# Attention with the projections inside its steps: the job order of the first layer's mixer

## The chip, the cores and the metric

The kernel runs on one NeuronCore of a Trainium2 chip, as one program that computes three layers for one sequence of 256 tokens. The metric is the device time of one execution in microseconds (us). The engines are named as in the profile: PE is TensorE (matrix products, with PEld for its weight loads), DVE is VectorE, ACT is ScalarE, POOL is GpSimd, and SP is SyncE, which here only issues transfers. All data are 32-bit floats; each matmul of the source is two matmul instructions in the trace, a transpose is one.

## What is computed

Only the first layer's mixer is touched. Its input is 256 x 1024, and one input matrix of 2840 columns gives all queries, keys, values and gates:

```python
def nsa_moba_mixer(x, positions, w_in, w_out, ...):
    proj = x @ w_in
    qa, kc, vc, ksl, vsl, kw, vw, ga, qm, km, vm = jnp.split(proj, EVEN_SPLITS, axis=-1)
    qa, kc, ksl, kw = (rope(...) for ...)              # 8 query heads, 2 key heads each
    gates = jax.nn.sigmoid(ga)                         # three a head
    o_a = nsa_attention(...)                           # o = g0 * o_cmp + g1 * o_slc + g2 * o_win
    o_b = moba_attention(rope(qm), rope(km), vm)       # 8 heads
    return jnp.concatenate([o_a, o_b], axis=-1) @ w_out
```

In nsa_attention, o_cmp attends to 15 compressed keys for each of two key heads, gelu((blocks + pos) @ w1) @ w2 over blocks of 32 tokens with a stride of 16. At 256 tokens the selected blocks, the sliding window and the block attention (moba) all come out as causal attention over all keys. So there are 24 causal attention jobs of 64 channels: 8 selected (slc), 8 sliding (win) and 8 block (moba). The mixer's output is added to alpha times its input and normalised; a mixture of experts (MoE) follows, and then two more layers with their own mixers and experts.

## The kernel before

**Weights.** SP streams all weights through six slots of 16 KB a partition (slot, free_slot, load_cols, load_out). Chunk n goes to slot n % 6 and may be loaded when chunk n - 6 has been used, which PE tells by chunk_done. Chunks 0 to 5 are the columns of w_in: 0 the NSA queries, 1 the keys and values kc, vc, ks, vs, 2 the window's keys and values and the gates (280 columns), 3 moba's queries, 4 its keys, 5 its values. Chunk 6 is the two compression matrices w1 (CMP_CHUNK, four DMAs with pieces of 512 B), 7 and 8 the two column halves of w_out, and from 9 on the experts of the first MoE. Between chunks 5 and 6, SP issues all the small parameters.

**Banks.** PSUM has eight banks of 128 x 512. project(n, ...) fills two of the banks 4 to 7, one for each tile t of 128 tokens, 8 products deep (KT = 8). ACT copies them out (take), DVE rotates queries and keys (rope), PE transposes them (tr, into banks 0 to 3), and ACT copies the transposed heads into qk. cmp_hidden forms the hidden layer of the compression.

**Attention.** The helper attention(jobs, first, pairs0, extras) is written once for each engine and goes through steps s = 0, 1, ... In step s, PE computes the scores of job s (bank s % 2), runs extras[s] if there is one, transposes the probabilities of job s - 3 (bank 2 or 3), and in every second step multiplies two jobs' probabilities by their values (bank 4 or 5 by the pair). DVE takes job s's masked minimum, scales job s - 1 by the inverse sum and the gate, and copies a pair's finished output to mixT. ACT computes the exponentials of job s and copies the transposed probabilities of job s - 3. Each engine works its list in order. AB_JOBS has the 8 moba jobs first, then slc and win, four jobs of a pair in a row; mixT tiles 0 to 3 are of the slc and win pairs, 4 to 7 of moba. The extras are the compression branch, which needs banks 6 and 7: hidden layer at step 2, its gelu, transpose, keys, scores at step 8, softmax, transpose at step 11. After the attention, project_out multiplies mixT by w_out into banks 4 to 7, and mixer_residual on DVE adds, takes the statistics and normalises.

**What orders PE.** First the input is transposed and projections 0 to 2 run; then tr(0) to tr(3), projection 3, tr(4), projection 4, the moba transposes, projection 5, the 28 steps, project_out. Projections 3, 4 and 5 stand between the NSA heads and the first step:

```python
project(3, 512, 3)
tr(4, [pj[:, t, C_KW:C_KW + P] for t in range(T)])
project(4, 512, 4)
project(5, 512, 5, moba_keys)
pe.wait_ge(qt_act, 7)
attention(AB_JOBS, 0, 0, {2: cmp_hidden, 6: cmp_hiddenT, 7: cmp_keys, 8: cmp_score, 11: cmp_transpose})
```

## Time and profile before

| | |
|---|---|
| median of 3 runs | 1370.96 us (1368.24 to 1385.06) |
| the profiled execution | 1370.9 us, span 1369.1 us |
| its mean granted TensorE clock | 0.932 of full speed |
| PE busy | 1240.8 us (91% of the span) |
| DVE, ACT busy | 319.1 us (23%), 204.4 us (15%) |
| HBM read | 362.60 MB, 266 GB/s over the span |
| chain that ended last | PE 73%, DMA 18%, DVE 4%, issue 2%, ACT 2% |

The page gives one profiled execution: busy time of each engine, the span in 40 slices of 34.2 us, the chain of work that ended last, the costliest groups. The trace behind it answers by stretch (windows), in order of time (timeline) and by what an engine waited for. PE's matmuls are pipelined and their ends are modelled, so a row's own duration overlaps the next by a little; the distance between two starts is what a piece of work takes. Between 0 and 203 us of the span lies the first mixer.

### The profile page before, as it was taken

The page shows a single profiled execution, that of the slowest core. Times are in us where ns is not written, and L with a number is a line of the kernel's source. Part 1 is how long each engine was busy: PE and PEld are TensorE (multiplying, and loading weights), DVE is VectorE, ACT ScalarE, POOL GpSimd, SP SyncE. Part 2 cuts the span into 40 slices and gives each one's busy share as a digit, 9 for nine tenths or more (in the row PEclk, how much of TensorE's full clock was granted, in tenths as well). Part 3 has the DMA queues.
Part 4 walks back from the last instruction along what each step waited for, and adds up shares of the span by engine and source line. Part 5 has one row for each costly group of instructions (what it writes and reads, how often), then busy time and mean ns, then how long its engine had stood idle before and what let it go on. Part 6 is the DMA issues. An engine that isn't in the chain of part 4 may idle for free.

```text
span 1369.1 us, 14568 instructions
## 1 busy us (share of the span) xinstructions
PE 1240.8 (91%) x5882; PEld 623.1 (46%) x5882; DVE 319.1 (23%) x891; ACT 204.4 (15%) x468; POOL 0.7 (0%) x5
## 2 busy tenths in 40 slices
PE   6999998999999998999799879898898999889885
PEld 3546546554477746554364454532242232233221
DVE  1324633121300534111502263510010010000002
ACT  2023502110101612010112122100000000000000
POOL 0000000000000000000000000000000000000000
PEclk9997798999999898999999958899999999999998
DMA  9772022999934011999653300269999999999993
GB/s 351 144 295 105 1 70 95 408 415 395 333 128 176 9 62 67 404 418 403 232 176 126 145 1 15 109 270 428 428 425 429 429 429 428 428 427 427 428 427 161
DMA packets 76872, 364.38 MB, mean 266 GB/s; under 512 B 21234, under 2 KB 26644, under 8 KB 52116
## 3 DMA queue, kind: packets, MB, share of 16 engines
q1 hardware_dynamic: 75876, 361.93, 66.3%
q10 hardware_dynamic: 944, 1.73, 0.4%
q8 instruction: 36, 0.59, 0.2%
q14 instruction: 16, 0.13, 0.0%
HBM read 362.60 MB, written 1.05 MB: 266 GB/s over the span
## 4 chain that ended last, share of the span: by engine, by line
PE 73%; DMA 18%; DVE 4%; issue 2%; ACT 2%; SPq 0%; DVEq 0%; ACTq 0%
DMA weights<-in_expert_w_down_dram 17%; PE bank L649 13%; PE bank L926 13%; PE bank L966 8%; PE bank L675 6%; PE bank L664 6%; PE bank L959 5%; PE bank L990 4%; PE bank L898 2%; PE bank L901 2%; PE bank L732 1%; PE bank L866 1%; PE bank L706 1%; DMA weights<-in_ab_w_in_dram 1%; PE bank L692 1%
## 5 line engine op out<-in xcount | busy, mean ns | idle before, releaser
L926 PE MATMUL bank<-weights,projected 128*64 128x256 f32 (+1 forms) x2048 | 344.2, 492 | 18.7 <-DMA weights<-in_expert_w_gate_dram 9.2
L926 PEld LDWEIGHTS bank<-weights,projected 128*64 128x64 f32 (+1 forms) x2048 | 135.1, 124 | 213.3 <-issue 170.0
L649 PE MATMUL bank<-weights,x_transposed 128*128 128x512 f32 (+1 forms) x416 | 178.9, 589 | 9.6 <-DMA weights<-in_ab_w_in_dram 6.3
L966 PE MATMUL bank<-weights,work 128*32 128x512 f32 x512 | 121.4, 629 | 30.3 <-DMA weights<-in_expert_w_down_dram 30.3
L649 PEld LDWEIGHTS bank<-weights,x_transposed 128*128 128x128 f32 x416 | 79.6, 194 | 101.5 <-issue 96.1
L966 PEld LDWEIGHTS bank<-weights,work 128*32 128x32 f32 x512 | 35.4, 115 | 113.8 <-issue 112.5
L675 PE MATMUL bank<-weights,mixed 128*128 128x512 f32 x192 | 83.2, 594 | 1.6 <-DVE mixed L1695 1.1
L664 PE MATMUL bank<-x_transposed,weights 128*128 128x256 f32 (+1 forms) x352 | 76.4, 379 | 0.0
L1881 DVE COPY work<-bank 128x512 f32<-128x512 f32 (+1 forms) x32 | 22.1, 690 | 209.8 <-PE bank L966 140.4
L664 PEld LDWEIGHTS bank<-x_transposed,weights 128*128 128x128 f32 (+1 forms) x352 | 63.8, 182 | 13.0 <-issue 1.3
L959 PE MATMUL bank<-weights,work 128*32 128x512 f32 x512 | 63.3, 626 | 1.6 <-DVE work L1886 1.6
L990 PE MATMUL bank<-work,heads_transposed 128*128 128x512 f32 x128 | 63.7, 620 | 0.0
L1901 DVE TENSOR_TENSOR work<-work,bank 64x512 f32<-64x512 f32 (+1 forms) x24 | 16.4, 682 | 187.1 <-PE bank L926 187.1
L1376 ACT ACTIVATE work<-bank 128x512 f32<-128x512 f32 (+1 forms) x32 | 19.0, 594 | 265.0 <-PE bank L966 195.0
L675 PEld LDWEIGHTS bank<-weights,mixed 128*128 128x128 f32 x192 | 36.2, 190 | 47.0 <-issue 44.5
L1271 ACT ACTIVATE projected<-bank 128x512 f32<-128x512 f32 (+1 forms) x34 | 18.1, 583 | 191.2 <-PE bank L649 140.2
L990 PEld LDWEIGHTS bank<-work,heads_transposed 128*128 128x128 f32 x128 | 21.0, 188 | 43.0 <-issue 38.3
L1886 DVE COPY work<-bank 128x256 f32<-128x256 f32 (+1 forms) x24 | 12.2, 509 | 114.7 <-PE bank L938 114.7
L1386 ACT ACTIVATE work<-bank 64x512 f32<-64x512 f32 (+1 forms) x24 | 14.1, 589 | 159.9 <-PE bank L926 159.9
L959 PEld LDWEIGHTS bank<-weights,work 128*32 128x32 f32 x512 | 14.9, 113 | 41.5 <-issue 38.8
L898 PE MATMUL bank<-heads_transposed,projected 128*128 128x128 f32 x256 | 31.9, 279 | 0.0
L901 PE MATMUL bank<-heads_transposed,projected 128*128 128x256 f32 x128 | 29.2, 382 | 3.0 <-issue 2.7
(282 smaller groups left out, 990.0 us busy)
## 6 DMA issues: line engine op xcount, KB each, us to landing
weights<-in_expert_w_gate_dram SPq DMA_DIRECT2D x32, 2048.0 KB, 15.6
weights<-in_expert_w_up_dram SPq DMA_DIRECT2D x32, 2048.0 KB, 17.3
weights<-in_expert_w_down_dram SPq DMA_DIRECT2D x32, 2048.0 KB, 17.2
weights<-in_moe_w_gate_dram SPq DMA_DIRECT2D x16, 2048.0 KB, 10.7
weights<-in_moe_w_up_dram SPq DMA_DIRECT2D x16, 2048.0 KB, 12.9
weights<-in_moe_w_down_dram SPq DMA_DIRECT2D x16, 2048.0 KB, 9.8
weights<-in_sb_w_in_dram SPq DMA_DIRECT2D x6, 2048.0 KB, 18.3
weights<-in_w_in_dram SPq DMA_DIRECT2D x6, 2048.0 KB, 15.0
```

Of the source, the lines that this page charges most:

```text
L649: i = mm(BANK[4 + 2 * (seq % 2) + t][:, 0:ncols], XT[:, kt, t * P:(t + 1) * P], w[:, kt, :], start=kt == 0, stop=kt == KT - 1)
L664: i = mm(BANK[4 + 2 * (seq % 2) + c // 2][0:width, (c % 2) * S:(c % 2 + 1) * S], w[:, kt, c * width:(c + 1) * width], XT[:, kt, :], start= ...
L675: i = mm(BANK[4 + 2 * half + t][:, :], mixT[:, kt, t * P:(t + 1) * P], w[:, kt, :], start=kt == 0, stop=kt == KT - 1)
L898: i = mm(to.rearrange("p (q t s) -> p q t s", t=T, s=cap)[:, :, t, :], XP[:, t, kt, :], place.rearrange("p (q s) -> p q s", s=cap), start= ...
L901: i = mm(to, XP[:, t, kt, :], place, start=t == 0, stop=t == T - 1)
L926: i = mm(b[n_slots * c:n_slots * (c + 1), e * F:(e + 1) * F], x[:, kt, q * n_slots:(q + 1) * n_slots], w[c][:, col:col + F], start=kt == 0 ...
L959: i = mm(BANK[2 + half][cap * q:cap * (q + 1), :], hT[:, e * step + f, s0:s0 + cap], slot(n + c)[:, col:col + CH], start=f == 0, stop=f == ...
L966: i = mm(BANK[2 + half][r0 + n_slots * c:r0 + n_slots * (c + 1), :], hT[:, a * step + f, n_slots * c:n_slots * (c + 1)], slot(n + c)[:, co ...
L990: i = mm(BANK[4 + 2 * t + half][:, :], w, YS[:, block % 2, half, :], start=False, stop=last and (SPLIT[L] or final))
L1271: i = ac(o, src, ACT.Copy, scale=scale)
L1376: ac(YS[r0:r0 + rows, (pair // 2 if rows < P else pair) % 2, 0, :], BANK[2][r0:r0 + rows, :], ACT.Copy).then_inc(y_act, 1)
L1881: cp(YS[r0:r0 + rows, (pair // 2 if rows < P else pair) % 2, 1, :], BANK[3][r0:r0 + rows, :]).then_inc(y_dve, 1)
```

## The change

The 16 slc and win jobs come first, then the 8 moba jobs; the pairs are renumbered so. SP loads the compression matrices as chunk 3 and moba's queries and keys as chunks 4 and 5, and moba's values as chunk 6 behind the small parameters. Ahead of the steps, PE now projects one tile of moba's queries, forms the hidden layer of the compression, with w1 as the stationary and the tokens as the moving operand (so it comes out transposed, and its transpose and copy are gone), and starts the other tile. The rest of moba's three projections is cut into pieces of two or four of the eight products and put in steps 0 to 9 and 14 to 17, through banks 6 and 7; its head transposes go to steps 10 to 13. The compression branch moves to steps 0 to 4 and to banks 4 and 5. The first six of the eight products of w_out's first half go to steps 20 to 24 and 26, into banks 6 and 7; the rest of it and the second half (banks 4 and 5) follow the steps. Since x_transposed stays in use, the probabilities' buffers that lay there move to the work and the norm buffers, as do the temporaries of the rotation, which is now done a tile at a time. The core of the diff:

```diff
-CMP_CHUNK = 6
+CMP_CHUNK = 3
...
-AB_JOBS = [("moba", h) for h in range(8)]
+AB_JOBS = []
 for _i in range(4):
     AB_JOBS += [("slc", 2 * _i), ("slc", 2 * _i + 1), ("win", 2 * _i), ("win", 2 * _i + 1)]
+AB_JOBS += [("moba", h) for h in range(8)]
 DIL_JOBS = [("dil", h) for h in range(8)]
 def job_pair(job):
     kind, h = job
-    return h // 2 + (4 if kind in ("slc", "win") else 0)
+    return h // 2 + (0 if kind in ("slc", "win") else 4)
...
+        AB_PR = PR[0:3] + [NORM_[:, 3072:3456]]
+        AB_PTS = PTS[0:2] + [WK[:, 3584:3968], WK[:, 3968:4352]]
+        AB_ROPE_TMP = [NORM_[:, 2048 + 256 * i:2048 + 256 * (i + 1)] for i in range(4)]
...
-            for c in range(6):
+            for c in range(3):
                 load_cols(N_AB + c, w, W_COL0[c], W_NCOLS[c])
+            cslot = slot(CMP_CHUNK).rearrange("p (v c n) -> p v c n", v=2, c=NC16)
+            for i, name in enumerate(("nsa_cmp_w1_k", "nsa_cmp_w1_v")):
+                for h in range(2):
+
+                    sp.dma_start(cslot[HD * h:HD * h + HD, i, :, :],
+                                 a[name][0][h * 1024:(h + 1) * 1024, :].rearrange("(c d) n -> d c n", d=HD)
+                                 ).then_inc(slot_loaded[CMP_CHUNK % NSLOT], 16)
+            for c in range(3, 5):
+                load_cols(N_AB + c + 1, w, W_COL0[c], W_NCOLS[c])
...
-            free_slot(CMP_CHUNK)
...
+            load_cols(N_AB + 6, w, W_COL0[5], W_NCOLS[5])
             load_norm(0, (a["ln_mix_g"][0], a["ln_mix_b"][0]))
...
+            HALF_FREE = {(N_AB + 4, 0): (proj_copied, 2), (N_AB + 4, 1): (proj_copied, 2),
+                         (N_AB + 5, 0): (half_copied, 1), (N_AB + 5, 1): (proj_copied, 4),
+                         (N_AB + 6, 0): (qt_act, 6), (N_AB + 6, 1): (qt_act, 7)}
+
+            def project_half(n, t, k0=0, k1=KT):
+
+                w = slot(n).rearrange("p (k c) -> p k c", k=KT)
+                if k0 == 0:
+                    pe.wait_ge(*HALF_FREE[n, t])
+                    chunk_loaded(n)
+                for kt in range(k0, k1):
+                    i = mm(BANK[6 + t][:, :], XT[:, kt, t * P:(t + 1) * P], w[:, kt, :], start=kt == 0, stop=kt == KT - 1)
+                if k1 == KT:
+                    i.then_inc(half_psum if t == 0 else chunk_done, 1)
...
+            def out_part(n, half, t, bank, kts=range(KT)):
+
+                chunk_loaded(n + half)
+                w = slot(n + half).rearrange("p (k c) -> p k c", k=KT)
+                for kt in kts:
+                    i = mm(BANK[bank][:, :], mixT[:, kt, t * P:(t + 1) * P], w[:, kt, :], start=kt == 0, stop=kt == KT - 1)
+                if kts[-1] == KT - 1 and t == T - 1:
+                    i.then_inc(chunk_done, 1)
+                elif kts[-1] == KT - 1 and half:
+                    i.then_inc(out_psum, 1)
...
+                    if jobs[j] == ("moba", 0):
+                        pe.wait_ge(qt_act, 7)
...
+                    if jobs[j - 1] == ("moba", 0):
+                        pe.wait_ge(proj_copied, 6)
...
-            project(3, 512, 3)
-            pe.wait_ge(roped, 3)
-            tr(4, [pj[:, t, C_KW:C_KW + P] for t in range(T)])
-            project(4, 512, 4)
-            pe.wait_ge(roped, 4)
-            for k in range(2):
-                tr(5 + k, [pj[:, t, C_QM + P * j:C_QM + P * (j + 1)] for j in (2 * k, 2 * k + 1) for t in range(T)])
-
-            def moba_keys():
-                pe.wait_ge(roped, 5)
-                for k in range(2):
-                    tr(7 + k, [pj[:, t, C_KM + P * j:C_KM + P * (j + 1)] for j in (2 * k, 2 * k + 1) for t in range(T)])
-
-            project(5, 512, 5, moba_keys)
-
+            project_half(N_AB + 4, 0)
...
             def cmp_hidden():
                 chunk_loaded(CMP_CHUNK)
                 pe.wait_ge(kv2_ready, 2)
-                pe.wait_ge(proj_copied, 6)
+                pe.wait_ge(proj_copied, 3)
                 for v in range(2):
                     kvv = kv2[:, v, :, :].rearrange("p h (n c) -> p (h n) c", c=NC16)
                     for c in range(NC16):
-                        i = mm(BANK[6][0:2 * NC16, v * P:(v + 1) * P], kvv[:, :, c], cw1[:, v, c, :],
-                               start=c == 0, stop=c == NC16 - 1)
+                        i = mm(BANK[5][:, v * 32:(v + 1) * 32], cw1[:, v, c, :], kvv[:, :, c], start=c == 0, stop=c == NC16 - 1)
                 i.then_inc(chunk_done, 1)
...
-            def cmp_hiddenT():
-                pe.wait_ge(hid_ready, 1)
-                for v in range(2):
-                    i = nc.tensor.transpose(BANK[7][:, v * 32:v * 32 + 2 * NC16], hid_g[0:2 * NC16, v * P:(v + 1) * P],
-                                            ident[0:2 * NC16, 0:2 * NC16])
-                i.then_inc(hidT_psum, 1)
...
+            def moba_heads(k):
+                pe.wait_ge(roped, 5 if k < 7 else 7)
+                col = C_QM if k < 7 else C_KM
+                j0 = 2 * ((k - 5) % 2)
+                tr(k, [pj[:, t, col + P * j:col + P * (j + 1)] for j in (j0, j0 + 1) for t in range(T)])
+
+            def out_first(kt):
+                pe.wait_ge(o_copied, kt + 1)
+                pe.wait_ge(half_copied, 3)
+                pe.wait_ge(proj_copied, 6)
+                for t in range(T):
+                    out_part(N_AB + 7, 0, t, 6 + t, range(kt, kt + 1))
+
+            cmp_hidden()
+            pe.wait_ge(roped, 3)
+            tr(4, [pj[:, t, C_KW:C_KW + P] for t in range(T)])
+            project_half(N_AB + 4, 1, 0, 4)
+            pe.wait_ge(qt_act, 3)
+            attention(AB_JOBS, 0, 0, {
+                0: lambda: project_half(N_AB + 4, 1, 4, 6),
+                1: lambda: (cmp_keys(), project_half(N_AB + 4, 1, 6, 8)),
+                2: lambda: (cmp_score(), project_half(N_AB + 5, 0, 0, 2)),
+                3: lambda: project_half(N_AB + 5, 0, 2, 4),
+                4: lambda: (cmp_transpose(), project_half(N_AB + 5, 0, 4, 6)),
+                5: lambda: project_half(N_AB + 5, 0, 6, 8),
+                6: lambda: project_half(N_AB + 5, 1, 0, 2),
+                7: lambda: project_half(N_AB + 5, 1, 2, 4),
+                8: lambda: project_half(N_AB + 5, 1, 4, 6),
+                9: lambda: project_half(N_AB + 5, 1, 6, 8),
+                10: lambda: moba_heads(5),
+                11: lambda: moba_heads(6),
+                12: lambda: moba_heads(7),
+                13: lambda: moba_heads(8),
+                14: lambda: project_half(N_AB + 6, 0, 0, 4),
+                15: lambda: project_half(N_AB + 6, 0, 4, 8),
+                16: lambda: project_half(N_AB + 6, 1, 0, 4),
+                17: lambda: project_half(N_AB + 6, 1, 4, 8),
+                20: lambda: out_first(0), 21: lambda: out_first(1), 22: lambda: out_first(2), 23: lambda: out_first(3),
+                24: lambda: out_first(4), 26: lambda: out_first(5)})
             pe.wait_ge(o_copied, 8)
-            project_out(N_AB + 7)
+            for t in range(T):
+                out_part(N_AB + 7, 0, t, 6 + t, range(6, KT))
+            for t in range(T):
+                out_part(N_AB + 7, 1, t, 4 + t)
...
+            def take_moba_half(c, t):
+
+                col = W_COL0[c]
+                take_half(N_AB + c + 1, t, pj[:, t, col:col + CH], -SCALE if c == 3 else 1.0, c - 2)
...
+            take_moba_half(3, 0)
+            act.wait_ge(hid_exp_in, 1)
+            ac(hid_t, hid_t, ACT.Exp, scale=-2.0 * float(np.sqrt(2.0 / np.pi))).then_inc(hid_exp, 1)
+            act.wait_ge(qt_psum, 5)
+            ac(qk[:, 5, :], BANK[0][:, 0:S], ACT.Copy).then_inc(qt_act, 1)
...
-            attention(AB_JOBS, 0, {4: gelu_exp, 6: hiddenT, 9: cmp_exponent, 11: cmp_pT_copy})
...
+            attention(AB_JOBS, 0, {2: lambda: (take_moba_half(3, 1), cmp_exponent()), 4: cmp_pT_copy, 6: lambda: take_moba_half(4, 0),
+                                   10: lambda: (take_moba_half(4, 1), moba_heads(5)), 11: lambda: moba_heads(6), 12: lambda: moba_heads(7),
+                                   13: lambda: moba_heads(8), 16: lambda: take_moba_half(5, 0), 18: lambda: take_moba_half(5, 1)})
...
+            def rope_moba(c, t):
+
+                dve.wait_ge(half_copied if t == 0 else proj_copied, c - 2 if t == 0 else c + 1)
+                rope_half(W_COL0[c], t)
+                dve.wait_ge(roped, 4 + 2 * (c - 3) + t)
...
+            link(cp(hid_g, BANK[5][:, 0:64]))
+            link(tt(hid_t, hid_g, hid_g, ALU.mult))
+            link(ts(hid_t, hid_t, 0.044715, 1.0, ALU.mult, ALU.add))
+            tt(hid_t, hid_t, hid_g, ALU.mult).then_inc(hid_exp_in, 1)
+            rope_moba(3, 0)
+            dve.wait_ge(hid_exp, 1)
+            link(ts(hid_t, hid_t, 1.0, None, ALU.add))
+            link(nc.vector.reciprocal(hid_t, hid_t))
+            tt(hidT, hid_g.rearrange("p (v n) -> p v n", v=2), hid_t.rearrange("p (v n) -> p v n", v=2), ALU.mult).then_inc(hidT_ready, 1)
...
-            attention(AB_JOBS, 0, 0, {3: gelu_in, 4: gelu_out, 7: keys_copy, 8: cmp_softmax_in, 10: cmp_softmax_out})
-            mixer_residual(N_AB + 7, 0, ALPHA, 0, "layer", X)
+            attention(AB_JOBS, 0, 0, {1: keys_copy, 2: cmp_softmax_in, 3: lambda: (cmp_softmax_out(), rope_moba(3, 1)), 7: lambda: rope_moba(4, 0),
+                                      11: lambda: rope_moba(4, 1)})
+            mixer_residual(N_AB + 7, 0, ALPHA, 0, "layer", X, banks=(6, 4))
```

## Rows read from the trace of the kernel before

**Rows 1.** The page's second part: 40 slices; granted clock in tenths of full speed.

```profile
PEclk9997798999999898999999958899999999999998
```

**Rows 2.** Windows: stretch, its length, busy of PE, PEld, DVE, ACT, POOL, PEclk, DMA, GB/s.

```profile
60.00:100.00 40.00, 40.00 (x113) 18.51 (x111) 8.91 (x16) 5.28 (x11) 0.00 (x0) 1.00 0.88 284
100.00:117.00 17.00, 13.81 (x103) 10.95 (x101) 9.29 (x39) 6.19 (x24) 0.00 (x0) 0.99 0.66 248
117.00:151.00 34.00, 32.66 (x132) 21.95 (x132) 17.46 (x83) 13.05 (x48) 0.00 (x0) 0.50 0.00 1
151.00:176.00 25.00, 22.82 (x149) 13.80 (x145) 15.69 (x77) 14.99 (x53) 0.00 (x0) 1.00 0.00 1
240.00:280.00 40.00, 40.00 (x325) 22.54 (x322) 7.87 (x13) 5.05 (x9) 0.00 (x0) 1.00 1.00 409
```

**Rows 3.** PE's timeline (start, us, line, count): projections 3 and 5, transposes, output projection.

```profile
55.86 13.90 PE L649 MATMUL bank<-weights,x_transposed 128*128 128x512 f32 x32
...
69.81 13.90 PE L649 MATMUL bank<-weights,x_transposed 128*128 128x512 f32 x32
83.55 1.04 PE L757 MATMUL bank<-consts,projected 128*128 128x128 f32 x8
84.42 7.03 PE L649 MATMUL bank<-weights,x_transposed 128*128 128x512 f32 x16
...
175.36 27.73 PE L675 MATMUL bank<-weights,mixed 128*128 128x512 f32 x64 [0.55 <-DVE mixed L1695]
```

**Rows 4.** What PE waited for, 55 to 205 us: total us, times, longest.

```profile
PE bank L732 <- ACT work L1325: 2.0, 1, 2.0
PE bank L732 <- ACT x_transposed L1325: 1.5, 4, 0.6
PE bank L834 <- DVE misc L1746: 1.1, 1, 1.1
PE bank L694 <- DVE misc L1682: 0.9, 1, 0.9
```

**Rows 5.** PE's timeline at the full clock: scores that open steps, and values behind them.

```profile
151.17 0.48 PE L694 MATMUL bank<-heads_transposed 64*128 64x128 f32 x2
...
154.22 0.87 PE L732 MATMUL bank<-x_transposed,projected 128*64 128x256 f32 x8 [0.32 <-ACT x_transposed L1325]
155.02 0.49 PE L694 MATMUL bank<-heads_transposed 64*128 64x128 f32 x2
...
158.91 0.48 PE L694 MATMUL bank<-heads_transposed 64*128 64x128 f32 x2
```

**Rows 6.** PE's timeline at the half clock: one step with values, and the next.

```profile
132.52 0.79 PE L694 MATMUL bank<-heads_transposed 64*128 64x128 f32 x2
...
136.41 0.79 PE L694 MATMUL bank<-heads_transposed 64*128 64x128 f32 x2
```

**Rows 7.** PE's timeline: hidden layer, compressed scores, the MoE's router, its residual.

```profile
101.78 7.20 PE L800 MATMUL bank<-weights,mixed 128*32 128x128 f32 x64
...
125.58 6.18 PE L828 MATMUL bank<-misc,heads_transposed 64*128 64x15 f32 x32
...
204.70 1.96 PE L856 MATMUL bank<-small_params,x_transposed 128*128 128x20 f32 x16 [0.73 <-ACT x_transposed L1260]
208.39 1.66 PE L625 MATMUL bank<-consts,residual 128*128 128x128 f32 x8 [1.72 <-DVE residual L1541]
210.99 3.57 PE L856 MATMUL bank<-small_params,x_transposed 128*128 128x20 f32 x16 [0.94 <-DVE x_transposed L1506]
214.39 6.02 PE L866 MATMUL bank<-residual,consts 128*128 128x512 f32 x8
```

**Rows 8.** DVE's timeline: token blocks, compressed softmax (first and last ops of its parts).

```profile
57.94 3.42 DVE L1641 TENSOR_TENSOR mixed<-bank,misc 64x256 f32<-64x256 f32 x8
...
131.80 0.76 DVE L1725 TENSOR_TENSOR projected<-bank,consts 128x256 f32<-128x256 f32 x2 [5.52 <-PE bank L828]
...
133.81 0.41 DVE L1734 TENSOR_TENSOR misc<-misc 128x240 f32<-128x240 f32 x1
...
139.44 0.42 DVE L1740 TENSOR_TENSOR misc<-misc,consts 128x256 f32<-128x256 f32 x1
...
141.05 0.42 DVE L1746 TENSOR_TENSOR misc<-misc 128x256 f32<-128x256 f32 x1
```

**Rows 9.** Windows of the start (columns as in rows 2): the first six chunks' loads.

```profile
20.00:40.00 20.00, 20.00 (x47) 8.88 (x46) 0.00 (x0) 1.08 (x2) 0.00 (x0) 0.97 1.06 383
40.00:60.00 20.00, 20.00 (x74) 12.35 (x73) 11.07 (x34) 3.00 (x7) 0.00 (x0) 1.00 0.53 40
```

136 lines of the change are left out of this document (58 added, 78 removed).

## The prediction

> **What bounds the kernel now.** I read the page first, then the windows of the first mixer, then PE's own timeline and waits there, and last the timelines of DVE and the transfers. The page gives one profiled execution of 1370.9 us, span 1369.1; the sum below is made against it, and it is as good as the median of the runs shown (1370.96). PE is busy 91% of the span and holds 73% of the chain that ended last. A busy PE is not a PE at full speed: the granted clock dips to 0.7 in the fourth and fifth slice [rows 1]. The windows show where [rows 2]. From 60 to 100 us, in the projections, PE is never idle at clock 1.00. From 100 to 117, in the first attention steps, it is busy 13.81 of 17 us. From 117 to 151 it runs at 0.50, that is 1.2 instead of 2.4 GHz. From 151 to 176 it is back at 1.00 and busy 22.82 of 25 us. So the stretch that the change touches, from the first instruction of projection 3 at 55.86 to the end of the output projection at 175.36 + 27.73 = 203.1, takes 147.2 us and is bound by PE, by PE's clock and by some short waits. The waits for ACT and DVE in it are 2.0, 1.5, 1.1 and 0.9 us [rows 4]; one more of 0.55 stands ahead of the output projection [rows 3]. What goes before 55.86 is not touched on PE.
>
> **What the change does to that stretch.** It takes nearly no product away and adds none: it puts dense products between thin ones. So I price all of PE's work from 55.86 at the full clock, add waits, and then ask where the clock would not be full.
>
> 1. Three input projections: projection 4 runs from 69.81 to 83.55, so 13.74 each [rows 3], 41.2 us. Cutting them in halves and pieces adds no instruction; a bank is kept open between pieces, and I take that as free, since the pieces have no wait of their own inside.
> 2. The hidden layer of the compression. Before, 64 matmuls with 32 columns of weights and 128 moving took 7.20 us [rows 7]. Now 64 with 128 columns of weights and 32 moving. The nearest row is the router, 16 matmuls with the same weights and 20 moving in 1.96 us, 0.122 each: 7.8 us. Bounds: the old 7.1, and 14.3 at the router's price at the half clock (3.57 / 16 = 0.223 each) [rows 7]. Its two transposes and one copy go, two small instructions on PE.
> 3. Head transposes: 8 take 83.55 to 84.42 = 0.87 [rows 3]; 16 for moba and 2 for the window's keys are 2.0 us.
> 4. The 24 jobs: two steps at full clock take 155.02 - 151.17 = 3.85, with 0.32 of wait in it, so 3.53 of work; with the product that opens a pair 3.89 [rows 5]. Twelve pairs of steps and four openings: 12 x 3.53 + 4 x 0.36 = 43.8 us.
> 5. Rest of the compression: 32 small score products took 6.18 at the half clock [rows 7], so 3.1; twelve other instructions at 0.122 are 1.5. Together 4.6 us.
> 6. Output projection: 27.6 us [rows 3].
>
> Sum of work: 41.2 + 7.8 + 2.0 + 43.8 + 4.6 + 27.6 = 127.0 us.
>
> **Waits.** The token blocks that the hidden layer needs are ready at 57.94 + 3.42 = 61.4 [rows 8]; PE comes there at 55.86 + 6.9 = 62.7, so nothing. The window's keys and the first gelu pass through DVE and ACT behind it, but PE has half a tile's projection (3.4 us) and its transposes meanwhile. The tightest place is steps 2 to 4: from the end of the compressed scores, DVE needs 2.4 us (131.80 to 134.2), ACT's exponential 0.4, DVE again 2.0 (139.44 to 141.45) [rows 8], and DVE's own step work, about 1.3, stands between: 6.1. PE has 2 x 1.7 of projection, two scores and a transpose, about 5.7: a wait of 0.4. Behind it on DVE stands one rotation of half a projection, six operations of 256 columns, 2.2 us by the 0.42 of such an op less its overlap [rows 8]; the minimum of job 4 is queued behind that, and PE asks for it only in step 6. In step 12 the last keys' rotation is asked for about a step after it can begin; I take 0.3 (bounds 0 and 2.2). ACT has four copies of projections and four of heads more in its steps; at 0.6 us they fit under PE's 1.8 to 3.5 us a step. At the end I keep 0.55 ahead of the output and 0.6 for ACT in the last steps. All waits: 1.85 us.
>
> **Transfers.** SP puts the four compression transfers ahead of moba's queries. By 40 us DMA moves 383 GB/s, from 40 to 60 only 40 [rows 9]: the six chunks are in by about 42. One chunk of 2 MB more in front is 5.5 us at that rate, and up to 10 if small pieces are slower; projection 3 wants its chunk at 55.86, so both ends are hidden. Moba's values come behind the small parameters and are wanted at step 14, past 105 us. Chunks 9 to 12 come free one by one in the steps, when DMA does nothing (1 GB/s from 117 to 176, rows 2); chunks 13 and 14 come free with the halves of w_out, 13.9 us ahead of the mixer's end and at it, as now. So the MoE that follows finds the same six slots in the same state and moves as a whole, although its own stretch is bound by DMA (share 1.00, 409 GB/s) [rows 2].
>
> With these terms the stretch takes 127.0 + 1.85 = 128.85 us and ends at 184.7 instead of 203.1: 18.4 us less, 1352.5 us.
>
> **The clock.** What can the engine be doing when the clock falls? Before 117 it had waited 2.0 us for ACT, with thin work around [rows 4]. Before 208.39 it had done only the router's 20-column products between waits of 0.73 and 1.72: the transposes at 208.39 take 1.66 for eight, and the router's second half has the half-clock price [rows 7]. The new hidden layer is the same kind of product, 7.8 us of it in a row, and nothing dense beside it. I take it that the clock falls in it once. The price: if it falls halfway, 32 matmuls x (0.223 - 0.122) = 3.2 us, and behind it dense products at the half clock until it is back: the residual's 8 products took 6.02 where 8 x 0.434 = 3.5 is the full-clock price [rows 3, 7], 2.5 us. Falling at its end costs 2.5 only, halfway 5.7; I take 4.1. Once in the steps 0 to 9, dense pieces hold it up. Forecast: 1352.5 + 4.1 = 1357 us.
>
> The Trainium skill, TensorE: Matmul & The Clock Gate, Part 4, says that transposes don't engage the full clock as other matmuls do. It would speak against steps 10 to 13, which lose their dense pieces and get four transposes each. From 151 to 176 plain steps, three transposes each, stay at 1.00 [rows 2], so the trace doesn't decide it.
>
> **Rivals.**
> - Clock stays full throughout: 1352.5 us. For it: plain steps keep 1.00 from 151 to 176, and the old hidden layer kept 0.99 in 100 to 117 [rows 2]. Against it: the router's rows. Chance 0.20.
> - The clock falls again, at the compressed scores (32 products of 15 columns, 3.1 us) or in steps 10 to 13: each such fall costs 2.5 at the next dense piece and about 2 in the thin work before it: 1361, twice 1366. Steps 10 to 13 are the page's rule as a mechanism; 4 x 2.3 us of thin work. Chance 0.25.
> - DVE or ACT sets the pace in the crowded steps 2 to 4 and 10 to 13, because several operations stand ahead of the minimum and the exponential: three waits of 2 us, 1359 to 1363. The rows leave DVE 1.3 us of a step's 3.5, so 0.06.
> - The change moves the mixer's end but not the kernel's, as the MoE waits for DMA anyway: 1371. It needs chunks that come late by the clock and not by a freed slot; DMA's rest from 117 to 176 speaks against it. 0.05.
> - The other side: the clock falls in the hidden layer and does not come back, as it did not for 34 us in the old steps although PE was busy 32.66 of them [rows 2]; one step with values then took 136.41 - 132.52 = 3.89 [rows 6]. Now dense pieces run in it too. Every microsecond at half clock loses half of itself, so from about 37 us of it the kernel is slower than before; if it lasted to the end of step 9 (42 us of full-clock work), 1397. Against it: the residual's dense products brought the clock back within 6 us [rows 7]. 0.04.
>
> **Numbers.** One fall has 0.40: likeliest, 1357. Bounds of its terms: -4 without it, +6.5 if the hidden layer runs cold throughout, +-2 for waits. The range that holds 8 in 10 is 1349 to 1367: it takes in the full clock, one and two falls and the waits, and leaves the unmoved end, three falls and the long cold out. About 2% (27 us) is what a measurement of this kernel tells from no change. The stretch holds 18.4 us in all, so faster by over 2% has 0.03, what my full-clock prices may miss; slower by over 2% only in the far end of the long cold, 0.02; within 2%, 0.95.
>
> **What would show it.** The output projection should end near 189 us. Clock 1.00 from about 80 us on, a dip near 66 to 76; no stretch of 30 us at 0.50. The hidden layer's 64 matmuls in 7.8 to 12 us. PE waits under 1 us each in the steps, the largest at the compressed transposes. The MoE's and later layers' lengths unchanged to a microsecond. A dip in steps 10 to 13 is the second rival; a mixer end near 189 with a total near 1371 is the fourth; a wait for DMA before 110 us makes the order of the transfers wrong.

## The result, and the profile after

| | before | after |
|---|---|---|
| median of 19 runs each | 1385.06 us (1368.24 to 1393.99) | 1362.41 us (1353.14 to 1374.87) |
| ratio | | 0.988, 95% interval 0.985 to 0.991 |
| the profiled execution | 1370.9 us, span 1369.1 | 1355.8 us, span 1354.0 |
| first mixer ends at | 202.9 us | 195.6 us |
| from there to the end of the span | 1166.2 us | 1158.5 us |

The change makes the kernel faster by 1.2% by the ratio, which is clear of the measurement and under the 2% that the prediction calls no change; the medians lie 22.7 us (1.6%) apart. Runs that lie over 1.5% above the fastest of their kernel (five of before's, one of after's) are left out of a ratio, and kept in a median. The forecast of 1357 lies beside the profiled 1355.8, but for a wrong reason: the last two lines say that half of the profiles' difference of 15.1 us lies behind the mixer, where nothing was changed. "Mixer's end" is here and below the start of the next transposes (L625 before, L633 after).

The granted clock by slices, from the page of after, beside [rows 1]: in place of the two slices at 0.7 (103 to 171 us) there is one, the third (68 to 102 us).

```profile
PEclk9979998999999898999999859899999999999998
```

Windows of the changed mixer, columns as in [rows 2]: two stretches at about half the clock, and 1.00 from 98 us to the end.

```profile
60.00:66.00 6.00, 6.00 (x31) 3.87 (x30) 2.19 (x6) 0.60 (x1) 0.00 (x0) 1.00 0.31 65
66.00:76.00 10.00, 10.00 (x48) 9.07 (x48) 1.67 (x7) 0.53 (x2) 0.00 (x0) 0.56 1.04 395
76.00:90.00 14.00, 14.00 (x69) 8.09 (x67) 5.97 (x27) 3.43 (x13) 0.00 (x0) 0.95 1.04 405
90.00:98.00 8.00, 8.00 (x14) 3.18 (x14) 5.69 (x21) 1.40 (x5) 0.00 (x0) 0.57 0.50 210
98.00:140.00 42.00, 40.95 (x192) 22.84 (x190) 23.44 (x104) 20.18 (x67) 0.00 (x0) 1.00 0.14 51
140.00:178.00 38.00, 35.93 (x166) 19.00 (x163) 13.03 (x65) 14.28 (x46) 0.00 (x0) 1.00 0.15 56
```

PE's timeline of after: hidden layer (L817), half of one tile's projection behind it (L687, eight products), compressed scores (L837), two pieces of four products behind them and one at the full clock, the output projection (L696, 40 products in a row from 178.28, which the views cut at 180 us) and the mixer's end (L633). From here on products are counted as the trace counts them: two to a product of the source.

```profile
63.65 10.47 PE L817 MATMUL bank<-mixed,weights 128*128 128x32 f32 x64
...
74.39 5.11 PE L687 MATMUL bank<-weights,x_transposed 128*128 128x512 f32 x8
...
86.77 3.32 PE L837 MATMUL bank<-misc,heads_transposed 64*128 64x15 f32 x32
90.02 2.78 PE L687 MATMUL bank<-weights,x_transposed 128*128 128x512 f32 x4
...
94.31 3.75 PE L687 MATMUL bank<-weights,x_transposed 128*128 128x512 f32 x4
...
102.43 1.98 PE L687 MATMUL bank<-weights,x_transposed 128*128 128x512 f32 x4
...
178.28 1.98 PE L696 MATMUL bank<-weights,mixed 128*128 128x512 f32 x4 [0.52 <-DVE mixed L1769]
179.67 16.04 PE L696 MATMUL bank<-weights,mixed 128*128 128x512 f32 x37
195.55 1.05 PE L633 MATMUL bank<-consts,residual 128*128 128x128 f32 x8
```

Four dense products take 1.98 us at the full clock and 3.75 at the half one. PE's waits in after (us in total, times, longest), beside [rows 4]:

```profile
PE bank L764 <- ACT work L1392: 1.8, 3, 0.8
...
PE bank L788 <- ACT projected L1330: 0.6, 1, 0.6
PE bank L696 <- DVE mixed L1769: 0.5, 1, 0.5
PE bank L788 <- DVE projected L1715: 0.5, 1, 0.5
```

And the part that no line of the change touches. First PE's timeline behind the second MoE of before, then the same place of after: the last products of the MoE, and the dense dummy products that keep the clock up (keep_clock_up).

```profile
656.58 2.01 PE L990 MATMUL bank<-work,heads_transposed 128*128 128x512 f32 x4
664.85 10.37 PE L639 MATMUL bank<-x_transposed,consts 128*128 128x512 f32 x18 [6.26 <-issue]
```

```profile
648.28 2.01 PE L1039 MATMUL bank<-work,heads_transposed 128*128 128x512 f32 x4
650.31 7.99 PE L647 MATMUL bank<-x_transposed,consts 128*128 128x512 f32 x18
```

Before, PE stands still for 6.26 us and waits for nothing that the profile shows; behind the stop the clock is down, so that the 18 products take 10.37 instead of 7.99. Together that is 8.6 us, of which 7.7 are left at the end of the span. The question of the experiments is thus double: what the mixer's gain is made of, and what the stop is.

### The profile page after: what moved, and what is told of

Its sections match the earlier page's. It is cut to its first block, busy times and chain, and to the rows that moved or that the text cites. A ratio compares the mean times of both kernels' runs of the same rounds, so it can differ in the third digit from the quotient of the medians.

```text
span 1354.0 us, 14585 instructions
## 1 busy us (share of the span) xinstructions
PE 1233.2 (91%) x5880; PEld 615.4 (45%) x5880; DVE 319.1 (24%) x903; ACT 205.4 (15%) x467; POOL 0.7 (0%) x5
## 4 chain that ended last, share of the span: by engine, by line
PE 73%; DMA 18%; DVE 5%; issue 1%; ACT 1%; SPq 0%; DVEq 0%; ACTq 0%
DMA weights<-in_expert_w_down_dram 17%; PE bank L975 13%; PE bank L657 10%; PE bank L1015 8%; PE bank L696 6%; PE bank L672 6%; PE bank L1008 5%; PE bank L687 4%; PE bank L1039 3%; PE bank L947 2%; PE bank L950 2%; PE bank L915 1%; PE bank L764 1%; DMA weights<-in_ab_w_in_dram 1%; PE bank L736 1%
## 5 line engine op out<-in xcount | busy, mean ns | idle before, releaser
L657 PE MATMUL bank<-weights,x_transposed 128*128 128x512 f32 (+1 forms) x320 | 137.8, 591 | 9.7 <-DMA weights<-in_ab_w_in_dram 6.4
L657 PEld LDWEIGHTS bank<-weights,x_transposed 128*128 128x128 f32 x320 | 61.8, 195 | 81.1 <-issue 75.7
L696 PE MATMUL bank<-weights,mixed 128*128 128x512 f32 x192 | 84.8, 597 | 1.6 <-DVE mixed L1769 1.0
L696 PEld LDWEIGHTS bank<-weights,mixed 128*128 128x128 f32 x192 | 35.7, 190 | 45.8 <-issue 43.3
L687 PE MATMUL bank<-weights,x_transposed 128*128 128x512 f32 x96 | 49.2, 652 | 0.0
L1320 ACT ACTIVATE projected<-bank 128x512 f32<-128x512 f32 (+1 forms) x28 | 14.8, 581 | 159.6 <-PE bank L657 108.7
L1756 DVE CUSTOM_DVE_ANT_0 work<-bank,consts 128x128 f32<-128x128 f32 (+1 forms) x64 | 21.3, 371 | 50.2 <-PE bank L725 41.9
```

The costliest lines, as they stand in the source:

```text
L657: i = mm(BANK[4 + 2 * (seq % 2) + t][:, 0:ncols], XT[:, kt, t * P:(t + 1) * P], w[:, kt, :], start=kt == 0, stop=kt == KT - 1)
L687: i = mm(BANK[6 + t][:, :], XT[:, kt, t * P:(t + 1) * P], w[:, kt, :], start=kt == 0, stop=kt == KT - 1)
L696: i = mm(BANK[bank][:, :], mixT[:, kt, t * P:(t + 1) * P], w[:, kt, :], start=kt == 0, stop=kt == KT - 1)
L1756: i = nc.vector.tensor_tensor_reduce(out=SM[J % 2][:, c0:c1], in0=BANK[J % 2][:, c0:c1], in1=const("unseen" if dil else "causal")[:, c0:c1 ...
```

## The experiments

The theories after the result. A: in the new mixer the clock falls twice, each time in a row of products with few moving columns (the hidden layer and the compressed scores). C: in the old one the thin steps don't bring the clock back in a fixed time, and dense work does. The rivals are named with each run. The ratios are to the kernel before, measured beside the run, with 95% intervals.

**The pair again**, before_again, after_again and before_third.

> The kernel before, unchanged, for a second profile. Mixer: output projection ends at 203 us within 1, in every profile. The first profile also has a 6.26 us stop of PE ahead of the first matmul behind the second MoE (line 639), which the kernel after does not have. Theory 1, the stop belongs to the program (where its instructions lie): it is there again, 6 us, and the span is near 1369. Theory 2, the stop is chance (instructions that arrive late among the weights' transfers): it is missing or has another size or place, and the span differs by as much.

> The changed kernel, unchanged, for a second profile. Output projection ends at 195.7 us within 1; the clock falls twice, in the hidden layer and at the compressed scores. Theory 1: no stop of PE behind the second MoE. Theory 2: it can be there, or elsewhere, and the span is longer by it.

> The kernel before, a third profile, for how long its half clock lasts. Theory C: it begins at 116 and ends at 150 (mixer end 203) or at 187 (mixer end 217), nothing fixed. Theory D: 150 again. One or two stops of 6 us behind a MoE.

Measured: 1381.6, 1353.7 and 1371.6 us; mixer's end at 202.9, 193.1 and 203.2. The changed mixer's clock falls twice again (the second time from 88 to 95), but its end is 2.5 us earlier than in the first profile and outside the 1 us that was expected. The rest behind the mixer is 1177.0, 1158.8 and 1166.5, with two, no and one stop of PE: at both MoEs (6.06 and 5.85), none, at the second (6.95). So the stop comes and goes with the execution.

**The hidden layer**, hid_wide: each product gets 128 moving columns by repeating the 32.

```diff
-    i = mm(BANK[5][:, v * 32:(v + 1) * 32], cw1[:, v, c, :], kvv[:, :, c], ...)
+    i = mm(BANK[5][:, v * P:(v + 1) * P], cw1[:, v, c, :], kvv[:, :, c].unsqueeze(1).to_broadcast([P, 4, 32]), ...)
```

> The changed kernel with the hidden layer's moving operand repeated four times, 128 columns instead of 32, the same 64 matmuls and weight loads; only the first 32 output columns are used. Theory A, the clock falls because the products are thin: it stays at 1.00 through the hidden layer, the 64 matmuls take 7.8 to 8.0 us instead of 10.3, the four products behind them 3.4 instead of 5.0, and the mixer ends about 4 us earlier, near 191.5. Theory B, it falls because of the weight loads or of the phase, whatever the width: the same 10.3 and 5.0 or more, and the mixer ends at 195.7 or later.

hid_old: the hidden layer as before the change, in its new place: the token blocks (32 columns) as weights, w1 moving with 128 columns, and the transposes and the copy behind it.

```diff
-    i = mm(BANK[5][:, v * 32:(v + 1) * 32], cw1[:, v, c, :], kvv[:, :, c], ...)
+    i = mm(BANK[5][0:2 * NC16, v * P:(v + 1) * P], kvv[:, :, c], cw1[:, v, c, :], ...)
...
+    def cmp_hiddenT():
+        pe.wait_ge(hid_ready, 1)
+        ...
-    1: lambda: (cmp_keys(), project_half(N_AB + 4, 1, 6, 8)),
+    1: lambda: (cmp_hiddenT(), project_half(N_AB + 4, 1, 6, 8), cmp_keys()),
```

> The changed kernel with the hidden layer in its old form (32 columns of weights, 128 contiguous moving columns, then two transposes and a copy) at its new place. The run with the operand repeated kept the clock at 1.00 but took 0.218 us a matmul, so width keeps the clock and the strided operand costs. Theory A, what streams matters: 64 matmuls in 7.2 us at clock 1.00, four products behind them in 3.4, mixer end near 192 in place of 193 to 196. Theory B, it falls whatever the form, by the work around it: the clock falls near 68 us and the mixer ends at 195 or later.

PE's timeline of hid_wide and of hid_old, hidden layer and half projection:

```profile
62.51 14.12 PE L817 MATMUL bank<-mixed,weights 128*128 128x128 f32 x64
76.69 3.60 PE L687 MATMUL bank<-weights,x_transposed 128*128 128x512 f32 x8
```

```profile
63.67 7.20 PE L819 MATMUL bank<-weights,mixed 128*32 128x128 f32 x64
71.08 3.60 PE L689 MATMUL bank<-weights,x_transposed 128*128 128x512 f32 x8
...
82.19 4.39 PE L846 MATMUL bank<-misc,heads_transposed 64*128 64x15 f32 x32
86.51 3.78 PE L689 MATMUL bank<-weights,x_transposed 128*128 128x512 f32 x4
```

Both take the first fall away: the eight products take 3.60 instead of 5.11. hid_wide pays for it with 14.12 (0.22 each, at the full clock) and gains nothing: median 1365.4 us, ratio 0.994 (0.989 to 0.998), mixer's end 196.8. hid_old keeps 7.20 and ends its mixer at 191.4, in 1359.4 us with one stop. The second fall stays in both. Theory A holds for the hidden layer in what it says of the clock, not in the time forecast for hid_wide, and the old form is the better one of the three.

**The compressed scores**, all_dense: hid_wide, and one pair of dense products of a projection ahead of the 32 score products and one after each of their first three quarters.

```diff
+                project_half(N_AB + 5, 0, 0, 1)
...
+                    if h in (1, 3, 5):
+                        project_half(N_AB + 5, 0, (h + 1) // 2, (h + 1) // 2 + 1)
```

> As hid_wide, and the compressed scores in step 2 have four dense products of the projection between them, one after every four (steps 3 and 4 carry two each, step 5 none). Theory A: the second fall, from 91 to 97 us, goes too, and the mixer ends about 3.5 us earlier than with hid_wide alone, near 188; about 0.995 of the time of the changed kernel. Theory B, the scores' fall has another cause (the transposes and waits of steps 3 and 4): the fall stays and the mixer ends as with hid_wide.

Windows of all_dense:

```profile
80.00:90.00 10.00, 10.00 (x42) 5.10 (x42) 4.29 (x22) 3.44 (x13) 0.00 (x0) 1.00 1.04 408
90.00:102.00 12.00, 12.00 (x38) 6.55 (x37) 3.15 (x13) 0.70 (x2) 0.00 (x0) 0.58 0.41 171
```

The fall comes all the same, and lasts longer than in after (90 to 98), with the mixer's end at 199.7 and a ratio of 0.993 (0.990 to 0.997). So pairs of dense products between the score products don't hold the clock, in this one profile; this part of A fell.

score_half: both key heads in one product. The keys are laid out block-diagonally, 128 rows by 32 columns, so that 16 products take the place of 32; the first fall is left as it is.

```diff
-    for h in range(8):
+    for n in range(4):
         for t in range(T):
...
-            i = mm(..., qk[r:r + HD, h % 4, t * P:(t + 1) * P], kcT[r:r + HD, 0:NBLK], start=True, stop=True)
+            i = mm(..., qk[:, n, t * P:(t + 1) * P], kcT, start=True, stop=True)
```

> The changed kernel with the compressed scores of two heads in one product (128 rows of weights, 32 moving columns, the compressed keys in two diagonal blocks): 16 matmuls instead of 32, about 1.7 us instead of 3.3. Theory A, the second fall needs some microseconds of thin work: it does not come, and the mixer ends 1.6 + 3 us earlier, near 191 (first fall as before). Theory B, it is the mix of steps 2 to 4 and not the scores: the fall comes within 5 us of the same place, and the end is 1.6 us earlier.

Windows of score_half, then its timeline: the first fall is there, the second is gone.

```profile
66.00:78.00 12.00, 12.00 (x48) 9.89 (x48) 3.74 (x13) 0.53 (x2) 0.00 (x0) 0.57 1.00 372
78.00:100.00 22.00, 21.61 (x90) 11.36 (x88) 14.45 (x62) 7.94 (x30) 0.00 (x0) 1.00 0.82 322
```

```profile
86.17 1.97 PE L835 MATMUL bank<-misc,heads_transposed 128*128 128x32 f32 x16
87.98 1.96 PE L687 MATMUL bank<-weights,x_transposed 128*128 128x512 f32 x4
```

1.97 us of score products instead of 3.32, dense products at 1.96 behind them, the mixer's end at 190.7, 2.4 and 4.9 us ahead of the changed kernel's two profiles; 1358.5 us, with one stop. best1 is hid_old and score_half together, best1_again the same once more.

> Both edits, hid_old and score_half. Theory A: clock 1.00 from 60 us to the mixer's end, which comes near 188; 0.996 of the changed kernel's time, 0.984 to 0.988 of before's. Theory B: one fall at least, end 192 or later.

> The changed kernel with the old form of the hidden layer and half as many compressed score products, once more. With 0, 1 or 2 stops and a mixer's end at 188 to 191 the runs lie at 1348 to 1351, 1357 to 1360 and 1364 to 1367 us; median 1356 to 1360, ratio to the kernel before 0.980 to 0.986, ahead of the changed kernel by 4 to 7 us.

best1: median 1355.8, ratio 0.984 (0.979 to 0.990), mixer's end 187.8, one fall of 4 us left. best1_again: 1361.4, ratio 0.987 (0.980 to 0.995), mixer's end 185.6. Both profiles had two stops of 5.6 to 6.0 us. It beats the kernel before; that it beats the changed one can't be seen through the stops, and needs best1_noif below.

The fall that is left in best1 lies at the merged scores, where score_half had none, and in best1_again the same code has none either. First best1's score products and the piece behind them, then best1_again's:

```profile
81.59 2.38 PE L844 MATMUL bank<-misc,heads_transposed 128*128 128x32 f32 x16
83.78 3.26 PE L689 MATMUL bank<-weights,x_transposed 128*128 128x512 f32 x4
```

```profile
81.12 1.97 PE L844 MATMUL bank<-misc,heads_transposed 128*128 128x32 f32 x16
82.93 1.96 PE L689 MATMUL bank<-weights,x_transposed 128*128 128x512 f32 x4
```

So half as many score products don't keep the clock up for certain: it falls there in two profiles of four (best1_noif, below, is the other), and the clock of 1.00 up to the mixer's end that best1's theory A gave came in best1_again alone. The old form of the hidden layer has kept it in all four profiles that have it. Whether a fall goes by the number of columns or by how long such a row lasts was not taken apart.

**How long the half clock lasts in the old order**, pad_b14 (28 waits that are fulfilled at once, ahead of PE's first instruction in the kernel before) and before_burst (before with eight dense dummy products, four of the source, in step 10, ahead of the compressed transposes).

```diff
+    for _ in range(28):
+        pe.wait_ge(first_consts_loaded, 16)
```

```diff
+    def burst():
+        pe.wait_ge(cmp_exp_in, 1)
+        for _ in range(4):
+            mm(BANK[7][:, :], ident, CONSTS[:, 0:CH], start=True, stop=True)
```

> The kernel before with 28 waits on an already raised semaphore in front of PE's first transpose (14 instructions of 64 bytes, while PE waits for the input anyway): they only shift all of PE's later instructions to where the changed kernel has them at the exits of the first two MoEs. The first profile of before has one stop of about 6 us at such an exit, the second has two, both profiles of the changed kernel none. Theory 1, the place of the instructions decides: the stops become rare as in the changed kernel, the fastest run is near 1362 instead of 1368 and the median about 0.994 of before. Theory 2, chance alone: the same times as before, fastest near 1370, median within 0.3%. In both the mixer ends at 203 us.

> The kernel before with four dense dummy products (128 columns of constants by 512, eight matmuls, 3.5 us at the full clock and 7 at the half) at attention step 10; their result is not used. In two profiles of before the half clock lasted from 116 to 150 us, in the shifted one from 116 to 187. Theory C, the thin steps of the old order cannot bring the clock back and chance decides how long it stays down; a dense run does: the clock is back by about 145 us, the mixer ends at 202 to 206 in the profile, and the times lose their slow upper group (median 0.99 to 1.00 of before, slowest run under 1387). Theory D, the clock comes back by its own time: same spread and the mixer 4 to 7 us longer, median 1.004.

Windows of pad_b14, then of before_burst:

```profile
117.00:151.00 34.00, 32.93 (x132) 21.98 (x132) 16.77 (x78) 13.05 (x48) 0.00 (x0) 0.50 0.00 1
151.00:185.00 34.00, 34.00 (x119) 19.99 (x120) 15.72 (x76) 13.73 (x51) 0.00 (x0) 0.50 0.00 0
```

```profile
117.00:140.00 23.00, 22.89 (x91) 15.89 (x92) 11.40 (x55) 8.32 (x31) 0.00 (x0) 0.50 0.00 0
140.00:145.00 5.00, 5.00 (x12) 2.22 (x12) 1.50 (x6) 0.37 (x1) 0.00 (x0) 0.66 0.00 2
145.00:176.00 31.00, 28.81 (x184) 17.45 (x183) 20.11 (x99) 19.46 (x70) 0.00 (x0) 1.00 0.01 1
```

The same code that had its clock back at 151 in [rows 2] keeps 0.50 for 36 us more in pad_b14, until 187, with PE busy 34.00 of the 34.00 us from 151 to 185; its mixer ends at 217.4, not at the 203 that was expected. The ratio, 0.998 (0.993 to 1.003), shows no effect of the place of the instructions, but it is no proof against one: theory 1's 0.994 lies in the interval, and the fastest of the ten runs, 1364.7, is under all of before's. The stop itself is still there, 6.07 us at the second MoE. With the burst the clock is back at 145 and the longest times are gone: none of ten runs is above 1380.7, where 14 of before's 19 beside it were (highest 1394.3); median 1376.8, ratio 0.997 (0.993 to 1.001). So dense work ends the half clock. It is not the only thing that does: at 151, and at 187 in pad_b14 (2.6 us ahead of the output projection), it ends in thin steps. What sets that time stays open. All three profiles of the unchanged kernel have the fall at 117 and the end at 151; the two profiles that last to 187 are of pad_b14 and before_noif (below), and there the fall shows about 2 us earlier, from 115.1 and 115.3. That the unchanged kernel has the long form too is read from its times: with its mixer's end at 203, two stops give 1381.6 (before_again), and 5 of its 19 runs lie above 1393.

**The parts of the change**, order_only (new order of jobs, moba's projections whole ahead of the steps, output projection whole behind) and out_last (the change, but the output projection whole behind).

```diff
-    10: lambda: moba_heads(5),
...
+    project_half(N_AB + 4, 1)
+    project_half(N_AB + 5, 0)
...
```

```diff
-    20: lambda: out_first(0), 21: lambda: out_first(1), 22: lambda: out_first(2), 23: lambda: out_first(3),
-    24: lambda: out_first(4), 26: lambda: out_first(5)})
...
-    out_part(N_AB + 7, 0, t, 6 + t, range(6, KT))
+    out_part(N_AB + 7, 0, t, 6 + t)
```

> The changed kernel's job order, transfers and compression branch, but all of the block attention's projections and head transposes ahead of the steps and all of the output projection behind them. Theory C: the reordering alone brings nothing: the compressed scores in step 2 let the clock fall and the thin steps do not bring it back for 30 us or more; the mixer ends at 200 us or later, up to 217; median 0.99 to 1.00 of before. Theory D, the gain is in the order and the earlier compression: it ends near 195 as in the changed kernel, 0.988.

> The changed kernel without output products in steps 20 to 26. Theory C: at the full clock PE is the bound, so moving them saves only waits that they cover; the waits of the last steps stay at about 2 us in all, and 12 cut products each cost about 0.1 us more when cut in pairs; the mixer ends within 1 us of 195.5 to 193. Theory D, they hold up the clock in the last steps: without them it falls after step 20 and the end is 4 us later or more.

order_only: median 1386.5 of ten runs (1369.1 to 1401.5), ratio 0.997 (0.992 to 1.001). Its profile has 0.50 from 120 to 160 and the mixer's end at 213.6. out_last: 1370.8 us with two stops, mixer's end 194.1, between the 193.1 and 195.6 of the changed kernel's two profiles, and the clock 1.00 from 100 to 190 us. So the pieces of output projection are worth nothing that one profile shows, and the gain comes with those of the input projections in steps 0 to 17.

**The stop.** Over all 20 profiles, the time from the mixer's end to the end of the span falls into three groups by the number of stops:

| stops of 5.6 to 7.0 us | profiles | us behind the mixer's end |
|---|---|---|
| none | 9 | 1155.3 to 1161.1 |
| one | 5 | 1166.1 to 1167.3 |
| two | 6 | 1171.8 to 1177.2 |

They stand only behind MoE 1 and MoE 2, where each engine jumps over the code for tokens that overflow their expert. after_noif leaves out, on all engines, the read of the overflow flag and the conditional block; after_flag leaves out the block alone; before_noif, best1_noif and order_only_noif are those kernels without both. No token overflows with these inputs.

```diff
-                flag = pe.value_load(OVER_I[0:1, 0:1], min_val=0, max_val=1)
-                with pe.If(flag > 0):
-                    ...
```

> The changed kernel without the overflow path of the first two MoEs: on every engine the read of the overflow flag and the conditional block behind it are left out (no token overflows with these inputs, so the block is jumped over anyway). Theory S: the stops of about 6 us ahead of the clock-keeping products behind MoE 1 and MoE 2 come from the jump over PE's conditional block. Then none is seen, the time behind the mixer's end is 1158 us in every execution, and the runs lie between 1350 and 1360 us, without the groups at 1362 and 1371 to 1375. Rival T: the stops come from the loads of weights that run at that moment, whatever PE's program does there: the runs still spread to 1371 to 1375, and a profile has a stop as often as before.

> The changed kernel with the read of the overflow flag kept on every engine and the conditional block left out. If the jump (the arrival of the instructions behind it) makes the stops, they are gone as in the run without both: runs within 1350 to 1360 us. If it is the read of the flag into a register that takes 6 us, they stay: groups near 1362 and 1371 to 1375.

> The kernel before without the flag's read and the conditional blocks. Theory S: behind the mixer's end 1158 us in every execution, runs at 1361 to 1363 us (mixer's end near 203) and, where the half clock lasts to the last steps, up to 1377; nothing at 1385 to 1394. The median then lies 7 to 10 us above that of the changed kernel without them, which is the mixer's own gain. Rival T: as the kernel before, 1369 to 1394 us.

> The changed kernel with the old form of the hidden layer and half as many compressed score products, and without the flag's read and the conditional overflow blocks of the first two MoEs (this part is left out). With the stops gone, 1158.4 us behind the mixer's end at 186 to 191 gives 1346 to 1351 us; that is 3 to 8 us under the changed kernel without the blocks (1354.1), which is what its two clock falls cost. If the falls cost nothing on average, because others take their place, it is 1354 as well.

> The new order of jobs with moba's projections whole ahead of the steps and the output projection whole behind them, and without the flag's read and the conditional overflow blocks of the first two MoEs (this part is left out). If the order alone brings nothing and only the dense pieces in the steps do, the runs lie where those of the kernel before without the blocks lie: 1364 to 1381 us or later, median about 1371, by how long the half clock lasts. If the order by itself helps, its median is near 1354 to 1360 us.

| | median us | lowest to highest | runs |
|---|---|---|---|
| before_noif | 1370.8 | 1363.7 to 1380.4 | 10 |
| order_only_noif | 1371.6 | 1360.9 to 1387.5 | 10 |
| after_noif | 1354.1 | 1351.7 to 1354.6 | 4 |
| after_flag | 1354.0 | 1349.5 to 1357.3 | 4 |
| best1_noif | 1345.95 | 1344.5 to 1348.7 | 6 |

The stops are gone, and with them the upper group of the changed kernel (8 of its 19 runs lay at 1370.8 to 1374.9). With the flag read and no block they are gone too, so it is the block and the jump over it, and not the read of the flag. Which engine's jump was not taken apart; the stop is seen on PE. What seems to be waited for are instructions; the profile has a queue of its own for them (packets, MB, share of 16 engines), though it doesn't say which engine it serves. First before in the stretch 662 to 665, just ahead of the restart at 664.85; then after in 646 to 648, ahead of its products at 650.31:

```profile
q8 instruction: 1, 0.02, 2.3%
```

```profile
q8 instruction: 1, 0.02, 2.9%
```

In before no such block lands from 648 to 662, and this one does between 662.0 and 662.8, 2.0 to 2.9 us ahead of PE's first product; at the two stops of before_again and the two of best1 it is 1.7 to 3.1 us, so in these five stops the restart follows the block. In after the block lands 2.5 to 3.4 us ahead of the same product, while PE is still at work on what it has queued. The Trainium skill, Runtime: NRT & Kernel Launch, Instruction fetch mechanics, says that a taken branch out of the fetched window forces a fetch before execution goes on. The traces fit this, and the stop is 5.6 to 7.0 us long, beside weights at 388 GB/s (658 to 664 us in before). That it is this fetch is argued from the block's time of landing; that the stops need the block of code is shown. Why the block comes in time in one execution and one such length late in the next was not found.

Windows of before_noif, of order_only_noif and of best1_noif:

```profile
120.00:185.00 65.00, 63.92 (x238) 40.00 (x239) 29.95 (x141) 23.92 (x87) 0.00 (x0) 0.50 0.00 1
```

```profile
120.00:134.00 14.00, 11.24 (x50) 7.72 (x51) 8.09 (x34) 4.76 (x17) 0.00 (x0) 0.52 0.08 32
134.00:180.00 46.00, 42.48 (x251) 25.27 (x248) 27.00 (x137) 25.81 (x93) 0.00 (x0) 1.00 0.00 1
```

```profile
60.00:80.00 20.00, 20.00 (x106) 12.47 (x106) 9.53 (x29) 3.35 (x12) 0.00 (x0) 1.00 0.75 259
80.00:90.00 10.00, 10.00 (x42) 5.92 (x40) 6.47 (x26) 2.87 (x10) 0.00 (x0) 0.83 1.05 403
90.00:187.00 97.00, 93.21 (x390) 49.11 (x391) 45.49 (x187) 34.79 (x115) 0.00 (x0) 1.00 0.24 92
```

Without stops the old order's times lie in three groups, 1364 to 1365, 1371 to 1373 and 1380, and the profile of the last group has the half clock until 187 us. The new order alone spreads more widely, from a profile with 14 us of half clock (1360.9) to 1387.5. Only the kernels with dense pieces in the steps lie within 8 us, in four to six runs each. From the medians: the change is worth 1370.8 - 1354.1 = 16.7 us, of it the order nothing (1371.6) and the dense pieces all. hid_old and score_half together bring another 1354.1 - 1345.95 = 8.2. That is not the price of the two falls: best1_noif still has one (the clock of 0.83 from 80 to 90), its merged scores save 1.3 us of work, and of the 10.1 us between the two profiles 6.1 lie in the mixer and 4.0 behind it.

## Why the prediction was right or wrong

**The class and the sign.** "Within 2%" held. That the kernel gets faster and that the mixer is bound by PE and its clock held too, and from step 4 on the clock stayed up as said. The forecast's 13.9 us against the profiled execution came out as 15.1, but as 7.4 in the mixer and 7.7 in a stop. The mixer's end was given as near 189 and is at 195.6 (193.1 to 193.7 in three other profiles of this mixer). The total near the profiled 1355.8 was luck: a mixer some 5 us longer than forecast and a stop that was missing made up for each other.

**The step that failed in the mixer** is "Once in the steps 0 to 9, dense pieces hold it up". They don't: the clock falls again at the compressed scores, in every one of the five profiles that have these scores and this hidden layer (after, after_again, after_noif, after_flag, out_last), and it costs about 4 us.

**The steps of the sum.** From 55.86 the forecast had 128.85 + 4.1 = 133 us; measured are 195.71 - 56.77 = 138.9, and a start 0.9 later, since projections 0 to 2 ran that much longer in this profile (after_again starts at 55.89).

- Input projections: 41.2 predicted, 47.0 measured. About 4.4 of the difference is half clock. The other 1.4 is the cutting that I took as free: at the full clock a piece of four products takes 1.82 us from start to start where four of an uncut row take 1.72, and a piece of eight 3.54 instead of 3.43. That bound was missing.
- Hidden layer: 7.8, and 10.3 with the fall. The row taken, the router's, was too dear: from 64 to 66 us 20 of its products ran at the full clock, 0.100 each. The fall itself cost 10.3 - 6.4 and 5.11 - 3.6 behind it, 5.4 where I had 4.1. That it would fall here, and once, was right, and the router's row was the right witness.
- Compressed scores: the second fall, which was the second rival's first place and not the forecast. 3.3 us of products, then 2.78 and 3.75 instead of 1.98 twice and two dear scores: about 4 us, near the 4.5 that the rival had. By its place it was the likelier case: the same kind of product as the hidden layer, which I had just argued to fall. I gave it 0.25 with "dense pieces hold it up" as the reason against, and all_dense shows that pairs of them between the scores don't.
- Steps 10 to 13 stayed at 1.00 (98 to 140 us), with seven transposes each among their other products. So the rule on transposes that I weighed (the Trainium skill, TensorE: Matmul & The Clock Gate, Part 4) is not borne out here as a mechanism.
- Waits: 1.85 predicted, 3.4 measured. The one at the compressed transposes (0.4) did not come at the slow clock and is 0.40 in score_half, where the clock is full. Two came in steps 11 and 12 (0.56, 0.49), and those for ACT in the last third of the steps came to 1.8 (0.81, 0.34, 0.67) where I had 0.6.
- Attention, rest of the compression, head transposes: 43.8, 4.6 and 2.0 predicted, about 43, 4.5 and 2.4 measured. Output projection 27.6 and 28.2, six pieces dearer by 0.1.
- Transfers: from the start of the new stretch (56.77) no wait for DMA before 110 us, as said.

**The step that failed for the total** is "it is as good as the median of the runs shown (1370.96)" together with "the MoE that follows ... moves as a whole". The profiled execution of before had one stop and its half clock ended early, at 151. Both vary from execution to execution: a stop costs 8 us in a part that I took as fixed, and the early end spares 14 us that others lose (mixer's end 217.4 in pad_b14 and 217.7 in before_noif). Over 19 runs the median of before is 1385, not 1371, and with no stop after and one before the profiles' difference held 7.7 us that the change has no part in. The rival "does not come back", which I gave 0.04 in the new order, is the old order's own state. With the dense pieces no profile has it: without stops the gain is 16.7 us of the medians, more than the forecast's 13.9 although the new mixer is some 5 us longer than forecast. The three runs shown (1368, 1371, 1385) held the hint: a spread of 17 us that my text did not ask about.

## What to carry to other kernels

Before pricing a change against one profile, ask of the spread of the times what varies: here the length of a half-clock stretch (up to 14 us) and stops at a jump (8 us each) were larger than the terms of the sum. Dense pieces between thin attention steps don't prevent a fall, and are worth their place because falls beside them were short. Look at rows of products with few moving columns first: turning the hidden layer round kept the clock in four profiles of four, merging two heads of scores into one block-diagonal product in two of four, and padding the operand cost more than the fall. A conditional block that is never taken is not free: its stops were 5.6 to 7.0 us here, with weights streaming beside them (without that traffic it was not tried).

## What the hardware showed that I had not expected

- A stop of 5.6 to 7.0 us of PE at a jump, with the clock down behind it: 18 dense products in 10.37 instead of 7.99.
- PE at 0.50 for 70 us although it was busy 34.00 of 34.00 us in half of them (pad_b14).
- The same 64 products of the hidden layer cost 0.100 each with 32 moving columns at the full clock, 0.112 as weights of 32 columns with 128 moving, and 0.22 with the 32 strided columns repeated to 128. The last moves no more columns than the second; the difference is in the moving operand's layout or its fourfold repeat, which was not taken apart.
- Cutting an accumulation into pieces costs 0.1 us a piece (1.82 instead of 1.72 for four products, 3.54 instead of 3.43 for eight).
- The same program, with the same merged scores, has a fall there in one execution (2.38 and 3.26 us, best1) and none in the next (1.97 and 1.96, best1_again).
